# Weight slots 64 bytes off the 1024-byte grid of the activations, in a two-layer streaming-encoder kernel

## The chip, the cores and the metric

The kernel runs on one core of a Trainium2 chip. The time is device time in microseconds (us), the median of several executions. Before the change it is 1166.72 us, the median of 3 runs (1166.25 to 1168.82). The engines go by short names in the profile: PE is TensorE, PEld its weight loads, DVE VectorE, ACT ScalarE, POOL GpSimd, SP SyncE (whose queue issues most DMAs).

## The reference

A trunk of two layers over 512 positions of width 1024, everything in float32. Layer 0 mixes with a short gated convolution beside a sliding-window attention, layer 1 with a gated spatial unit beside a latent attention; each layer then has a SwiGLU feed-forward network (FFN) of hidden width 2816. Cut to its frame:

```python
for layer in range(DEPTH):                       # 2
    h = rmsnorm(x, mix_norm[layer])
    z = h @ (e_w_in if layer % 2 == 0 else o_w_in)[layer // 2]
    ...                                          # conv + window attention, or gating + latent attention
    y = jnp.concatenate([rmsnorm(ya, ...), rmsnorm(yb, ...)], axis=-1) @ w_out
    x = x + y
    h = rmsnorm(x, ffn_norm[layer])
    gate, up = jnp.split(h @ w_ffn_in[layer], 2, axis=-1)     # 1024 x 5632
    x = x + (jax.nn.silu(gate) * up) @ w_ffn_out[layer]       # 2816 x 1024
```

## The kernel before

Activations lie in SBUF with the feature on the partition and the 512 positions along the row, as tiles of 128 x 512 float32 (2048 bytes a row). Every large matrix product is made of three products of split numbers: a value is kept as `hi`, rounded to the type float32r, and `lo`, the rest, also float32r. `product` (lines 1505 to 1509) then adds hi x hi, hi x lo and lo x hi in the same PSUM bank. With the weights as the stationary operand (128 x 128) the moving one is a 128 x 512 tile of activations; in the loads `O_CV` and in the value half of `O_UKV` the roles are the other way round.

Weights come in 188 numbered loads of up to 1024 columns a row. For each, SyncE issues a DMA into one of two `raw` slots; ScalarE copies it, rounded, into one of four slots of `w_hi` (`hi`, line 651); VectorE subtracts and writes the same slot of `w_lo` (`lo`, line 1039); TensorE then uses it, in `load` (mostly 24 matmuls), and counts `load_used`, which frees the slot for load n + 4. ScalarE and VectorE each have their order of work written out by hand, with `through(p)` as the places at which splits are made. In the FFN (`ffn_in`, `ffn_out`) these are loops on every engine.

Other matmuls work in plain float32: `mean` (line 1538) sums squares over partitions with `ones` or a block matrix as the stationary operand, transposes (lines 1545, 1606, 1897, 1959) take the identity from the tile `small`, and the scores and values of the attentions are at lines 1596, 1618, 1882 and 1908.

Where tiles lie: `place[0]` begins at a multiple of 1024 bytes, and `sb` takes the next free place and rounds the size up to a multiple of 64. The order is xT, h_hi, h_lo, raw, w_hi, w_lo, then small, tables, gains, mix0_gain, gate_bias, sinks, eps_col, spare, mask_q, mask_k, tiny. Behind `tiny` the place is rounded up to a multiple of 1024 and row_scale, acc, sq, y0, rs follow; then, from R, the activations of the stages at offsets of whole kilobytes. The slots of `w_hi` and `w_lo` are 4096 bytes a row, so all of them begin at a multiple of 1024, and a stationary slice in them at a multiple of 512:

```python
base = (nc.sbuf_base + 1023) // 1024 * 1024
...
    place[0] += (n + 63) // 64 * 64
...
place[0] = (place[0] + 1023) // 1024 * 1024
row_scale = sb("row_scale", [P, S])
```

Of the kernel before, what the change touches and what calls it, by code (L numbers as in the profile page):

```python
# [106 lines left out]
def program(nc, x, mix_norm, ffn_norm, w_ffn_in, w_ffn_out, e_w_in, e_conv, e_q_gain, e_k_gain,  # L107
# [6 lines left out]
    place = [base]  # L114

    def at(name, shape, dt, offset):
        return nc.alloc_sbuf_tensor_at(name, shape, dt, offset=offset)

    def sb(name, shape, dt=F32, size=4):
        n = size  # L120
        for d in shape[1:]:
            n *= d
        t = at(name, shape, dt, place[0])
        place[0] += (n + 63) // 64 * 64
        return t
# [6 lines left out]
    out_tok = at("out_tok", [P, QT, D], F32, h_at)  # L132

    raw = sb("raw", [P, RAW_SLOTS, 1024])
    w_hi = sb("w_hi", [P, W_SLOTS, 1024], F32R)
    w_lo = sb("w_lo", [P, W_SLOTS, 1024], F32R)

# [1887 lines left out]
```

## Time and profile before

| | before |
|---|---|
| median of 3 runs | 1166.72 us (1166.25 to 1168.82) |
| profiled execution | 1169.08 us, span of the trace 1167.3 us |
| granted TensorE clock, mean | 0.993 |
| PE busy | 1135.6 us, 97% of the span |
| PEld busy | 904.8 us, 78% |
| DVE busy | 579.3 us, 50% |
| ACT busy | 440.7 us, 38% |
| POOL busy | 118.2 us, 10% |
| HBM read, written | 101.23 MB, 2.10 MB |

The profile is one execution. A matmul's record holds its way through the array too, so records overlap, and the busy time of PE says less than how far apart matmuls start. The ends of matmuls are modelled.

### The profile page before, as it was taken

What the parts mean: (1) busy time and instruction counts of PE and PEld (TensorE: products, weight loads), DVE (VectorE), ACT (ScalarE), POOL (GpSimd) and SP (SyncE); (2) the same over time, 40 slices, a digit from 0 to 9 for tenths busy, and PEclk for the clock granted to TensorE, in tenths of its full rate; (3) what the DMA queues carried; (4) which work ended last, traced back from release to release, by engine and by line L of the source; (5) the groups of instructions that cost most, each with busy time, mean ns of one, the idle gap of its engine ahead of it and who ended that gap; (6) DMA issues with size and microseconds to landing.
All of it is one profiled execution on the core that took longest, in us unless ns stands there. A gap on an engine that the chain in (4) does not pass through costs nothing.

```text
span 1167.3 us, 13729 instructions
## 1 busy us (share of the span) xinstructions
PE 1135.6 (97%) x5059; PEld 904.8 (78%) x5059; DVE 579.3 (50%) x796; ACT 440.7 (38%) x681; POOL 118.2 (10%) x154
## 2 busy tenths in 40 slices
PE   6999889999999999999999989999999999999998
PEld 5777678888888888888877745588888888888886
DVE  6578885533434433242665796565343343342321
ACT  5445444423323322131546666543332332331210
POOL 5010200001101000000204120000110110110000
PEclk9999999999999999999999998999999999999999
DMA  6522123233223232232323210023323323322230
GB/s 186 190 56 71 55 74 107 82 98 107 89 92 107 90 96 103 90 101 79 91 75 93 72 40 16 1 72 109 95 89 105 99 89 99 106 87 95 90 126 36
DMA packets 84983, 103.87 MB, mean 89 GB/s; under 512 B 10579, under 2 KB 61456, under 8 KB 84816
## 3 DMA queue, kind: packets, MB, share of 16 engines
q1 hardware_dynamic: 81792, 101.99, 28.0%
q10 hardware_dynamic: 2096, 1.05, 0.3%
q8 instruction: 25, 0.41, 0.2%
q0 software_dynamic: 1056, 0.30, 0.1%
q14 instruction: 14, 0.11, 0.0%
HBM read 101.23 MB, written 2.10 MB: 89 GB/s over the span
## 4 chain that ended last, share of the span: by engine, by line
PE 91%; DVE 6%; ACT 1%; DMA 1%; issue 1%; POOL 0%; ACTq 0%; DVEq 0%; POOLq 0%
PE ps L1507 27%; PE ps L1509 27%; PE ps L1508 27%; PE ps L1882 2%; PE ps L1538 2%; PE ps L1908 2%; DMA x_tok<-in_x 1%; PE ps L1897 1%; DVE e_sc L1188 1%; DVE e_pT L1196 1%; PE ps L1884 0%; DVE e_sc L1177 0%; DVE conv_y L1237 0%; DVE rs L1091 0%; PE ps L1959 0%
## 5 line engine op out<-in xcount | busy, mean ns | idle before, releaser
L1039 DVE TENSOR_TENSOR w_lo<-raw,w_hi 128x1024 fp32r<-128x1024 f32 (+2 forms) x194 | 227.9, 1180 | 445.2 <-ACT w_hi L651 442.1
L651 ACT ACTIVATE w_hi<-raw 128x1024 fp32r<-128x1024 f32 (+2 forms) x194 | 196.1, 1017 | 486.5 <-PE ps L1509 471.0
L1507 PE MATMUL ps<-h_hi,w_hi 128*128 128x512 f32 x928 | 368.2, 397 | 0.6 <-DVE conv_h L1208 0.6
L1509 PE MATMUL ps<-h_hi,w_lo 128*128 128x512 f32 x928 | 362.1, 390 | 0.0
L1508 PE MATMUL ps<-h_lo,w_hi 128*128 128x512 f32 x928 | 362.0, 390 | 0.0
L1507 PEld LDWEIGHTS ps<-h_hi,w_hi 128*128 128x128 f32 x928 | 174.9, 188 | 41.5 <-issue 4.6
L1508 PEld LDWEIGHTS ps<-h_lo,w_hi 128*128 128x128 f32 x928 | 174.9, 188 | 38.3 <-issue 2.6
L1509 PEld LDWEIGHTS ps<-h_hi,w_lo 128*128 128x128 f32 x928 | 174.6, 188 | 36.6
L1507 PE MATMUL ps<-act_hi,w_hi 128*128 (+1 forms) x352 | 137.1, 390 | 0.0
L1509 PE MATMUL ps<-act_hi,w_lo 128*128 (+1 forms) x352 | 137.1, 389 | 0.0
L1508 PE MATMUL ps<-act_lo,w_hi 128*128 (+1 forms) x352 | 137.0, 389 | 0.0
L544 POOL TENSOR_TENSOR ffn_t<-ffn_t,row_scale 128x512 f32<-128x512 f32 x40 | 50.9, 1293 | 555.6 <-ACT ffn_t L816 555.6
L1508 PEld LDWEIGHTS ps<-act_lo,w_hi 128*128 128x128 f32 x352 | 66.1, 188 | 13.8
L1507 PEld LDWEIGHTS ps<-act_hi,w_hi 128*128 128x128 f32 x352 | 66.1, 188 | 13.7
L1509 PEld LDWEIGHTS ps<-act_hi,w_lo 128*128 128x128 f32 x352 | 66.1, 188 | 13.6
L1291 DVE TENSOR_TENSOR ffn_t<-ps,ffn_t 128x512 f32<-128x512 f32 x44 | 30.4, 692 | 44.7 <-POOL ffn_t L544 40.7
L819 ACT ACTIVATE act_hi<-ffn_t 128x512 f32 (+1 forms) x44 | 27.9, 633 | 49.2 <-DVE ffn_t L1291 49.2
L816 ACT ACTIVATE ffn_t<-ffn_t 128x512 f32<-128x512 f32 x44 | 27.1, 632 | 39.0 <-DVE ffn_t L1287 39.0
L1294 DVE TENSOR_TENSOR act_lo<-ffn_t,act_hi 128x512 f32 (+1 forms) x44 | 30.2, 687 | 6.5 <-ACT act_hi L819 6.3
L1882 PE MATMUL ps<-o_k,o_q 128*128 128x512 f32 (+3 forms) x64 | 27.7, 517 | 4.6 <-ACT o_p L971 3.1
L1263 DVE TENSOR_TENSOR xT<-ps,xT 128x512 f32<-128x512 f32 x32 | 20.9, 684 | 19.4 <-PE ps L1509 19.4
L1287 DVE TENSOR_TENSOR ffn_t<-ps,row_scale 128x512 f32<-128x512 f32 x44 | 28.2, 682 | 0.0
(247 smaller groups left out, 1079.7 us busy)
## 6 DMA issues: line engine op xcount, KB each, us to landing
raw<-in_w_ffn_in SPq DMA_DIRECT2D x88, 512.0 KB, 3.5
raw<-in_w_ffn_out SPq DMA_DIRECT2D x44, 512.0 KB, 3.7
raw<-in_e_w_in SPq DMA_DIRECT2D x18, 512.0 KB, 3.6
raw<-in_o_w_in SPq DMA_DIRECT2D x8, 512.0 KB, 3.6
raw<-in_o_w_out SPq DMA_DIRECT2D x8, 512.0 KB, 3.6
raw<-in_e_w_out SPq DMA_DIRECT2D x8, 256.0 KB, 3.8
raw<-in_e_w_out SPq DMA_DIRECT2D x4, 512.0 KB, 3.9
out_dram<-out_tok SPq DMA_DIRECT2D x8, 256.0 KB, 3.6
```

The lines of the kernel that those rows point to most:

```text
L544: pool.tensor_tensor(ffn_t[:, t, :], ffn_t[:, t, :], row_scale[:, :], ALU.mult).then_inc(silu_scaled, 1)
L651: ins = act.activation(dst, src, ACT.Copy)
L816: act.activation(ffn_t[:, b, :], ffn_t[:, b, :], ACT.Silu).then_inc(silu_done, 1)
L819: act.activation(dst[:, t, :], ffn_t[:, (t0 + t) % 4, :], ACT.Copy).then_inc(hidden_hi, 1)
L1039: ins = TT(dst, src, high, ALU.subtract)
L1287: TT(ffn_t[:, (t0 + t) % 4, :], ps[:, b0 + t, :], row_scale[:, :], ALU.mult).then_inc(gate_scaled, 1)
L1291: TT(ffn_t[:, b, :], ps[:, b0 + 2 + t, :], ffn_t[:, b, :], ALU.mult).then_inc(hidden_ready, 1)
L1294: TT(dst_lo[:, t, :], ffn_t[:, (t0 + t) % 4, :], dst_hi[:, t, :].bitcast(F32), ALU.subtract).then_inc(hidden_lo, 1)
L1507: MM(dst, st_hi, mv_hi, start=start, stop=False)
L1508: MM(dst, st_hi, mv_lo, start=False, stop=False)
L1509: return MM(dst, st_lo, mv_hi, start=False, stop=stop)
L1882: MM(s_, o_q[:, h, i * P:(i + 1) * P], o_k[:, h, 0:P * (i + 1)], start=True, stop=False)
```

## The change

One line is added to the function that places the tiles: the place moves on by 64 bytes between `raw` and `w_hi`. `w_hi`, `w_lo` and the tiles that follow them up to `tiny` begin 64 bytes later; `row_scale` and all behind it stay, since the rounding ahead of it takes up the 64 bytes.

```diff
     raw = sb("raw", [P, RAW_SLOTS, 1024])
+    place[0] += 64
     w_hi = sb("w_hi", [P, W_SLOTS, 1024], F32R)
     w_lo = sb("w_lo", [P, W_SLOTS, 1024], F32R)
```

## Rows read from the trace of the kernel before

**Rows 1.** The page: busy times, then the chain by engine and by line.

```profile
PE 1135.6 (97%) x5059; PEld 904.8 (78%) x5059; DVE 579.3 (50%) x796; ACT 440.7 (38%) x681; POOL 118.2 (10%) x154
...
PE 91%; DVE 6%; ACT 1%; DMA 1%; issue 1%; POOL 0%; ACTq 0%; DVEq 0%; POOLq 0%
PE ps L1507 27%; PE ps L1509 27%; PE ps L1508 27%; PE ps L1882 2%; PE ps L1538 2%; PE ps L1908 2%; DMA x_tok<-in_x 1%; PE ps L1897 1%; DVE e_sc L1188 1%; DVE e_pT L1196 1%; PE ps L1884 0%; DVE e_sc L1177 0%; DVE conv_y L1237 0%; DVE rs L1091 0%; PE ps L1959 0%
```

**Rows 2.** One line's instructions, line 1509: launches, ns min/median/max, first and last start.

```profile
L1509 PE MATMUL ps<-h_hi,w_lo x928: 387/389/628, 16.2 to 1037.5; 128*128 128x512 f32 x186
...
L1509 PE MATMUL ps<-w_hi,h_lo x32: 388/390/398, 594.0 to 618.8; 128*128 128x512 f32 x32
...
L1509 PE MATMUL ps<-ckv_hi,w_lo x8: 387/389/396, 664.7 to 681.8; 128*128 128x512 f32 x8
```

**Rows 3.** Busy time by stage, PE alone: window, us, busy (count), clock, DMA.

```profile
250.00:520.00 270.00, 270.00 (x1193) 1.00 0.31 97
820.00:1080.00 260.00, 260.00 (x1149) 1.00 0.31 95
```

**Rows 4.** Instructions in order of time, steady FFN: start us, us, engine, line.

```profile
300.68 0.39 PE L1508 MATMUL ps<-h_lo,w_hi 128*128 128x512 f32 x1
300.68 0.19 PEld L1509 LDWEIGHTS ps<-h_hi,w_lo 128*128 128x128 f32 x1
```

**Rows 5.** Single matmuls by line (85.9, 1158.9, 669.6 us), and the weight load after 85.94.

```profile
L1508 PE MATMUL ps<-h_lo,w_hi 128*128 128x512 f32 x1 | 0.4, 390 | 0.0
L1509 PE MATMUL ps<-h_hi,w_lo 128*128 128x512 f32 x1 | 0.4, 388 | 0.0
...
L1508 PE MATMUL ps<-act_lo,w_hi 128*128 128x512 f32 x1 | 0.4, 389 | 0.0
L1509 PE MATMUL ps<-act_hi,w_lo 128*128 128x512 f32 x1 | 0.4, 389 | 0.0
...
L1508 PE MATMUL ps<-w_lo,ckv_hi 128*128 128x256 f32 x1 | 0.3, 283 | 0.0
L1509 PE MATMUL ps<-w_hi,ckv_lo 128*128 128x256 f32 x1 | 0.3, 279 | 0.0
...
88.71 0.50 PEld L1606 LDWEIGHTS ps<-small,e_sc 128*128 128x128 f32 x3 [2.80 <-issue]
```

**Rows 6.** Plain float32: lines 1538 and 1897 by tile, two means in order of time.

```profile
L1538 PE MATMUL ps<-acc,small x20: 589/591/668, 32.5 to 808.7; 128*128 128x512 f32 x20
L1897 PE MATMUL ps<-small,o_p x80: 272/273/332, 692.4 to 749.5; 128*128 128x128 f32 x80
...
209.11 1.02 PE L1538 MATMUL ps<-acc,small 128*128 128x512 f32 x2
```

**Rows 7.** After a plain matmul at 209.56: two of eight matmuls in order, one by line.

```profile
210.20 0.40 PE L1508 MATMUL ps<-h_lo,w_hi 128*128 128x512 f32 x1
...
211.82 0.39 PE L1509 MATMUL ps<-h_hi,w_lo 128*128 128x512 f32 x1
...
L1509 PE MATMUL ps<-h_hi,w_lo 128*128 128x512 f32 x1 | 0.4, 397 | 0.0
```

**Rows 8.** VectorE and ScalarE by line: launches, ns min/median/max, first and last start.

```profile
L1230 DVE SCALAR_TENSOR_TENSOR conv_y<-conv_h,gains,conv_y x4: 742/743/746, 123.0 to 125.0; 128x511 f32<-128x511 f32 x4
L1102 DVE SCALAR_TENSOR_TENSOR yb<-yb,gains,rs x4: 743/748/752, 147.8 to 153.5; 128x512 f32<-128x512 f32 x4
L1039 DVE TENSOR_TENSOR w_lo<-raw,w_hi x194: 685/1226/1842, 12.6 to 1138.7; 128x1024 fp32r<-128x1024 f32 x170, 128x512 fp32r<-128x512 f32 x12, 128x768 fp32r<-128x768 f32 x12
L651 ACT ACTIVATE w_hi<-raw x194: 611/1061/1070, 11.5 to 1137.6; 128x1024 fp32r<-128x1024 f32 x170, 128x512 fp32r<-128x512 f32 x12, 128x768 fp32r<-128x768 f32 x12
```

**Rows 9.** The start in order of time, and the DMA issues by line (KB, us to landing).

```profile
0.76 0.40 SPq L373 DMA_DIRECT2D small<-const_small  x1
7.03 3.46 PE L1545 MATMUL ps<-small,x_tok 128*128 128x128 f32 x16 [7.03 <-DMA x_tok<-in_x]
...
small<-const_small SPq DMA_DIRECT2D x1, 128.0 KB, 3.4
```

## The prediction

> **What bounds the kernel now.** I read the chain that ended last first: TensorE is 91% of it, and the three matmul lines of `product` carry 27% each, VectorE only 6% [rows 1]. So what the change can be worth is decided by one number, how far apart two of those matmuls start. The view of line 1509 counts them: its ten groups, from 928 launches down to 8, add up to 1488; lines 1507 and 1508 are issued beside it each time, so 4464 launches in all, nearly all with 512 columns [rows 2]. Next, the busy time by stage: 270 us of the first FFN hold 1193 matmuls and 260 us of the second 1149, each count including two that begin before the window, at full clock with no idle [rows 3]. That is 270 / 1191 = 226.7 ns and 260 / 1147 = 226.7 ns from start to start. 512 columns at 2.4 GHz are 213.3 ns, so 13.3 ns of each interval are not columns: 4464 x 13.3 = 59 us of the kernel. Whether these 13.3 ns have to do with where the operands lie is the whole question.
>
> In this stretch the load of the next stationary tile begins together with a matmul's stream: the load at 300.68 with the matmul at 300.68, and so on, 0.19 us long [rows 4]. Both then read SBUF. The stationary tile is a slice of a weight slot, the moving one a tile of the activations. Before, slots and activations all begin at multiples of 1024 bytes and slices step by 512 bytes, so the two reads begin 0 or 512 bytes apart modulo 1024; after, 64 or 576.
>
> **The change, part by part.** No instruction, wait or transfer is added, removed or put in another order. What moves by 64 bytes is w_hi, w_lo and all that `sb` places behind them down to `tiny`: the constants with identity and ones, tables, gains, the bias and sink tiles, the masks. The tail behind `w_lo` has 576 bytes modulo 1024, with the 64 it has 640, and the rounding ahead of `row_scale` takes up both: from `row_scale` on every address is the same.
>
> The weight load against the stream. The test is a matmul beside which no weight load runs. At 85.94 us a 512-column one ends its weight slot's work, and the next weight load comes at 88.71 us: it lasts 388 ns, the one before it, with a weight load beside it, 390. At 1158.93 us, again with nothing behind it, it is 389 after 389. With 256 columns, the last of its stage lasts 279 ns, the one before it 283 [rows 5]. A collision of the two reads is thus worth 0 to 2 ns in a 512-column stream and some 4 ns in a 256-column one, not 13. Where do the 13 come from? They belong to this kind of matmul, and an address of the stationary tile has nothing to do with them. The rest, 2 to 3 ns, is about what lies between two plain fp32 matmuls: two of them take 1.02 us together, the second begins 1.02 - 0.59 = 0.43 us after the first, for 0.427 us of columns [rows 6].
>
> So the gain is bounded by 1.5 ns (389.5 against 388) on 4464 matmuls, 6.7 us, if 64 bytes end all collision; by 4 ns, 18 us, if the 256-column case is the true size of it. The trace also has the other side. After a pause or a plain matmul the intervals are longer for a while: from 210.20 us to 211.82 us seven of them take 1.62 us, 231.4 ns each, and one of these matmuls lasts 397 ns; then the 226.7 ns return [rows 7]. The addresses in those eight are the same as in the steady stretch, so what differs is how the two streams stand to each other in time. If the shift kept them in that state, each interval would cost 4.8 ns more: 4464 x 4.8 = 21 us. I take nothing for either: zero is nearest to the long stretches, in which tiles 0 and 512 bytes apart follow each other and two engines write in between, and 1191 intervals in a row have one length.
>
> Here the Trainium skill can be weighed. SBUF — State Buffer, section "Who interferes with whom", gives TensorE two independent read ports and says that it never waits for anyone; by it the sum is zero. The 283 against 279 ns do not agree to the last nanosecond, by which the page's zero and the 18 us above differ; no row tells whether those 4 ns hang on the address.
>
> The engines that write the slots. In the FFN a load is 24 matmuls or 5.4 us of TensorE, and its split is one ScalarE copy of 1.06 us and one VectorE subtraction of 1.23 us [rows 8]: even if both took twice as long, TensorE would hide them. In the first 200 us and around the attention VectorE stands in the chain with 6%. There an operand that begins 4 bytes off costs nothing: 743 ns for 511 elements at line 1230, against 748 ns for 512 aligned ones at line 1102 [rows 8]. Zero, and if each subtraction for the 26 loads ahead of the first FFN lost 10 ns, 0.3 us.
>
> The constants as moving or stationary operands: transposes read the identity, the means the ones, at 64 instead of 0 or 512. The largest group, 80 transposes at line 1897, would move by 0.4 us at 5 ns each [rows 6]; the others are smaller.
>
> The transfers into shifted tiles: the first, 128 KB of `small`, is issued at 0.76 us and lands 3.4 us later, at 4.2; TensorE starts at 7.03 us when x arrives [rows 9]. 2.8 us of cover; without it, a start that is late by a few tenths. The tables are used 600 us later. Nothing.
>
> Sum: 0 us, against the profiled execution's 1169.1 us (span 1167.3 and 1.8 around it), which is 2.4 us over the median of the three runs; on the median, 1166.7 us.
>
> **The rivals.** First: the shift does end collisions, a little. For it: 279 against 283 ns. Against it: 388 against 389 and 390, and that 0 and 512 bytes make no difference now. 4.5 to 18 us less, 1149 to 1162 us.
>
> Second: the 13.3 ns are a conflict of two reads that begin alike, after all, and the lone matmul only looks as long since the ends of matmuls are modelled. Then an interval would fall to the overhead of a plain matmul, 3 ns over its columns: 10 ns x 4464 = 45 us, 1122 us. Against it: with weights as the moving operand the median is 390 ns, with weights as the stationary one 389 [rows 2], whichever of the two reads is the one from the slot. The Trainium skill, TensorE: Matmul & The Clock Gate, section "Back-to-back issue gap", has 2.5 ns over the columns for a warm matmul, where this trace has 13.3; taken as a rule for this kind too it would put the gain at 10.8 ns x 4464 = 48 us.
>
> Third, the slower side: place, the intervals inside every load; mechanism, a stationary tile that begins 64 bytes further meets the faster stream a little later, and the even pace of 226.7 ns gives way to that after a restart. Price 4.8 ns x 4464 = 21 us, 1188 us, or 1 to 1.5 ns and 1171 to 1173 us when only the collisions double. It decides from the point at which an interval in the FFN is longer than 227.2 ns (2.3 us over the kernel). Against it: the record of a weight load is 0.19 us long in 0.227 us, so it isn't what an interval waits for [rows 4].
>
> That the change does nothing it says is no rival: the addresses do move.
>
> **How the numbers follow.** No difference 0.64, with its own range of 1164.4 to 1169.1 us. First rival 0.14 (0.09 of it above 1160 us), second 0.05, third 0.17 (0.08 of it up to 1174 us). A measurement of this kernel can tell about 0.2% (2.3 us) from no change: faster 0.19, same 0.64, slower 0.17. The range from 1160 to 1174 us holds 0.64 + 0.09 + 0.08 = 0.81.
>
> **What would show it.** In the profile after, 270 us of the first FFN should hold 1193 matmuls again; 1198 or more would mean that collisions cost and are gone, 1188 or fewer the third rival. The 512-column records should keep their median of 389 ns, the weight loads 188, and the lone one 388. Two intervals that alternate between even and odd slices (0 and 512 bytes) would show an effect of the address even where their sum stays. The prediction is wrong at its root if the lone record and the interval shrink together: then the 11 ns were not this matmul's own.

## The result

The changed kernel takes 1193.91 us (median of 4 runs, 1193.43 to 1194.37) against 1167.77 us for the kernel before in the same comparison (4 runs): a ratio of 1.0224, 95% interval 1.0212 to 1.0236. It is slower by 26 us, outside the range of the prediction. Place and sign are those of its third rival: every interval inside the loads is longer.

The profiled execution after took 1193.57 us with a span of 1191.8 us, 24.5 us over the span before. (The profiled execution before was 1.3 us over its own median, so this difference is smaller than the 26 us between the medians.) The page after, engines and chain (all line numbers are one higher than before), to be held against [rows 1]:

```profile
PE 1161.2 (97%) x5059; PEld 904.7 (76%) x5059; DVE 579.4 (49%) x796; ACT 440.8 (37%) x681; POOL 118.6 (10%) x154
...
PE 90%; DVE 6%; ACT 2%; DMA 1%; issue 1%; POOL 0%; ACTq 0%; DVEq 0%; POOLq 0%
```

The instruction counts are the same, DVE, ACT and PEld are as busy as before to within 0.1 us, and PE alone has 25.6 us more. Nobody waits for anything new. The busy time by stage, PE alone, the windows of [rows 3]:

```profile
250.00:520.00 270.00, 270.00 (x1158) 1.00 0.30 93
820.00:1080.00 260.00, 260.00 (x1115) 1.00 0.30 94
```

There were 1193 and 1149 matmuls in these windows. One of the 1158 began before its window: 270 / 1157 = 233.4 ns from start to start, and 233.3 from the single starts, against 226.7. Of the 1115 two did: 260 / 1113 = 233.6 ns, a little more because this window now holds the two plain matmuls of a mean, at 822.64 us, and the restart behind them. The single matmuls in order of time, start and length in us, in the steady first FFN:

```profile
299.76 0.40 PE L1508 MATMUL ps<-h_hi,w_hi 128*128 128x512 f32 x1
300.00 0.39 PE L1509 MATMUL ps<-h_lo,w_hi 128*128 128x512 f32 x1
300.23 0.40 PE L1510 MATMUL ps<-h_hi,w_lo 128*128 128x512 f32 x1
300.47 0.39 PE L1508 MATMUL ps<-h_hi,w_hi 128*128 128x512 f32 x1
...
302.10 0.40 PE L1509 MATMUL ps<-h_lo,w_hi 128*128 128x512 f32 x1
```

Records of 0.40 and 0.39 us take turns: in nanoseconds 398 and 393, with intervals of 236 and 231, over and over, 233.3 ns in the mean. From 300.00 to 302.10 us there are nine intervals. (At the end of the second FFN every record is 394 and every interval 233 or 234, the same mean by another pattern.) Before, the records were 389 or 390 and every interval 226 to 228.

Where the 24.5 us lie, from the first matmuls of the loads that bound each stage, in order of time in both traces:

| stage | before, us | after, us | more |
|---|---|---|---|
| up to the end of the first output projection | 198.2 | 200.2 | 2.0 |
| first FFN, 1584 matmuls | 359.9 | 370.5 | 10.5 |
| odd layer's input projections | 106.0 | 107.8 | 1.7 |
| attention, second part | 85.3 | 84.1 | -1.2 |
| second output projection | 47.9 | 48.9 | 1.0 |
| second FFN, 1584 matmuls | 361.5 | 372.0 | 10.5 |

1584 x 6.67 ns are 10.6 us: each FFN is explained to 0.1 us by the interval alone. All 4464 at that price would be 29.8 us; outside the FFNs less is lost, and the traces show several reasons, whose shares were not separated. Part of the loss disappears in waits. Before, the restarts after pauses had longer intervals than 226.7 ns already. And in the four loads in which the weights are the moving operand the interval is not 233 ns but, once settled, 228.9, here eight intervals in 1.83 us:

```profile
608.94 0.39 PE L1508 MATMUL ps<-w_hi,h_hi 128*128 128x512 f32 x1
...
610.77 0.39 PE L1510 MATMUL ps<-w_hi,h_lo 128*128 128x512 f32 x1
```

There the stationary slice lies 64 bytes below the moving tile, which is 192 modulo 256; the experiments below find the same 228.9 ns at 192 bytes.

The -1.2 us of the attention can't be put down to the addresses. In both executions TensorE's clock fell to its lower level, 1.2 GHz, in this stage. Ahead of the fall TensorE had been waiting part of the time (before it was busy for 3.8 of 6.0 us, after for 12.2 of 16.8). Two windows around the low clock, before and then after; the third figure from the end is the granted clock, which makes some 10 us at the lower level before and 7 us after:

```profile
696.00:707.00 11.00, 10.11 (x20) 0.53 0.15 48
...
712.80:719.70 6.90, 6.90 (x15) 0.51 0.20 76
```

### The profile page after: what moved, and what is told of

Its sections match the earlier page's. It is cut to its first block, busy times and chain, and to the rows that moved or that the text cites. A ratio compares the mean times of both kernels' runs of the same rounds, so it can differ in the third digit from the quotient of the medians.

```text
span 1191.8 us, 13729 instructions
## 1 busy us (share of the span) xinstructions
PE 1161.2 (97%) x5059; PEld 904.7 (76%) x5059; DVE 579.4 (49%) x796; ACT 440.8 (37%) x681; POOL 118.6 (10%) x154
## 4 chain that ended last, share of the span: by engine, by line
PE 90%; DVE 6%; ACT 2%; DMA 1%; issue 1%; POOL 0%; ACTq 0%; DVEq 0%; POOLq 0%
PE ps L1508 27%; PE ps L1510 27%; PE ps L1509 27%; PE ps L1883 2%; PE ps L1539 2%; PE ps L1909 1%; DMA x_tok<-in_x 1%; DVE e_sc L1189 1%; PE ps L1898 1%; ACT e_sc L740 1%; DVE e_sc L1178 1%; DVE tiny L1170 1%; PE ps L1885 0%; DVE e_pT L1197 0%; DVE conv_y L1238 0%
## 5 line engine op out<-in xcount | busy, mean ns | idle before, releaser
L1508 PE MATMUL ps<-h_hi,w_hi 128*128 128x512 f32 x928 | 373.1, 402 | 0.6 <-DVE conv_h L1209 0.6
L1510 PE MATMUL ps<-h_hi,w_lo 128*128 128x512 f32 x928 | 367.2, 396 | 0.0
L1509 PE MATMUL ps<-h_lo,w_hi 128*128 128x512 f32 x928 | 367.2, 396 | 0.0
L1508 PEld LDWEIGHTS ps<-h_hi,w_hi 128*128 128x128 f32 x928 | 174.7, 188 | 47.2 <-issue 4.6
```

The source lines that it names most:

```text
L1508: MM(dst, st_hi, mv_hi, start=start, stop=False)
L1509: MM(dst, st_hi, mv_lo, start=False, stop=False)
L1510: return MM(dst, st_lo, mv_hi, start=False, stop=stop)
```

## The experiments

Three theories were open. **A**: the distance between the stationary slice and the moving tile decides. **B**: a weight slot off the 1024-byte grid is slow by itself. **C**: other engines or the shifted constants are the cause.

### Whole kernels: constants alone, everything alike

```diff
     w_lo = sb("w_lo", [P, W_SLOTS, 1024], F32R)
+    place[0] += 64
```

> The 64 bytes are put behind w_lo instead of ahead of w_hi: only the constants and small tiles move, the weight slots stay on the 1024-byte grid. If the weight slots are the cause (theories A and B), the time is that of before, 1166 to 1169 us, and the FFN interval 226.7 ns. If the shifted identity, ones, tables or gains were the cause, it is that of after, about 1194 us.

Measured: 1167.98 us, ratio 1.0005 (0.9994 to 1.0016); 1193 matmuls in the 270 us window. Moving identity, ones, tables and gains costs nothing that can be measured.

```diff
-    base = (nc.sbuf_base + 1023) // 1024 * 1024
+    base = (nc.sbuf_base + 1023) // 1024 * 1024 + 64
...
-    place[0] = (place[0] + 1023) // 1024 * 1024
+    place[0] = (place[0] + 959) // 1024 * 1024 + 64
```

> Everything is shifted by 64 bytes, weight slots and activations alike, so that the distance between them is 0 or 512 modulo 1024 as before, and both begin at 64. Theory A (the distance decides): 1166 to 1169 us, interval 226.7 ns. Theory B (slots off the grid are slow by themselves): about 1194 us, interval 233.3 ns.

Measured: 1169.08 us, ratio 1.0012 (1.0000 to 1.0024), the window again:

```profile
250.00:520.00 270.00, 270.00 (x1193) 1.00 0.32 97
```

The slots are off the grid as in the changed kernel, and the time is that of before. B has fallen, and so has any theory about where ScalarE and VectorE write the slots: what decides is the distance between slots and activations.

### Whole kernels: other distances

The same one-line edit as the change, with another number of bytes.

> Slots 192 bytes off the grid: 228.9 ns in TensorE alone. Theory A, the full kernel has the same interval: 4464 x 2.2 = 10 us more, 1175 to 1179 us. If the grid of 1024 bytes decided (theory B): as after, 1194 us.

> Slots 256 bytes off the grid. Theory A with a period of 256 bytes, as TensorE alone showed it: the time of before, 1166 to 1169 us. With a period of 1024 bytes: between the two.

> Slots 128 bytes off the grid. TensorE alone has 232.4 ns there for one offset, 233.3 with slices 512 bytes apart in one of two runs of the stretch. If the interval alone sets the time (theory A): 1187 to 1194 us, FFN interval 232.4 to 233.3 ns. Theory B (only 64 is bad): 1167 us.

```diff
     w_hi = sb("w_hi", [P, W_SLOTS, 1024], F32R)
+    place[0] += 64
     w_lo = sb("w_lo", [P, W_SLOTS, 1024], F32R)
```

> Only the slots of w_lo are 64 bytes off, those of w_hi stay on the grid. In TensorE alone with the lo slices 64 bytes apart from the hi ones the mean interval was 231.1 ns. Theory A (each matmul pays by the distance of the slice that is loaded beside it, with what the one before left over): 231.1 ns, 4464 x 4.4 = 20 us more at most, 1182 to 1187 us. If each launch paid by its own slice alone, one in three would be at 233.3: 228.9 ns and 1175 to 1177 us.

The windows of 250 to 520 us with the slots at 192, 256 and 128 bytes and with w_lo alone at 64, in this order:

```profile
250.00:520.00 270.00, 270.00 (x1181) 1.00 0.30 95
...
250.00:520.00 270.00, 270.00 (x1192) 1.00 0.31 97
...
250.00:520.00 270.00, 270.00 (x1164) 1.00 0.30 92
...
250.00:520.00 270.00, 270.00 (x1170) 1.00 0.30 94
```

| slots at, bytes | FFN interval from the single starts, ns | time, us | ratio (95% interval) |
|---|---|---|---|
| 64 (the change) | 233.3 | 1193.91 | 1.0224 (1.0212 to 1.0236) |
| 128 | 232.4 | 1191.46 | 1.0205 (1.0176 to 1.0235) |
| 192 | 228.9 | 1174.79 | 1.0066 (1.0049 to 1.0083) |
| 256 | 226.7 | 1167.03 | 0.9999 (0.9987 to 1.0011) |
| w_lo alone at 64 | 231.1 | 1185.37 | 1.0153 (1.0124 to 1.0183) |

Three of the four times came where expected; with 192 bytes the interval did, and the time is 7.8 us over its comparison instead of 10, just under the stated band; as with the change, less is lost outside the FFNs. What counts is the distance modulo 256 bytes, not 1024. With w_lo alone, a third of the stationary slices is shifted and the kernel pays 18 us of the 26: the launches don't pay each for itself.

### TensorE alone: the distance

A kernel in which TensorE alone multiplies split tiles of x, 72 matmuls for each distance, after one plain fp32 matmul. The rest of the computation is left out. Its core (one such line for each stretch):

```diff
+        for o, st, mv, f, l in plan(64, 0, 1024, 512): ins = MM(o, st, mv, start=f, stop=l)
```

> This kernel leaves the whole computation out: TensorE alone multiplies split tiles of x, in 33 stretches of 72 matmuls in the order of product(), with a plain fp32 matmul between stretches; only the byte offsets of the stationary slices (s) and of the moving tile (m) differ. First 16 stretches: all slices at one offset, s = 0, 64, ... 960 modulo 1024, m = 0. Then 12 with slices stepping by 512 bytes as in the kernel, s = 0, 16, 32, 48, 64, 96, 128, 192, 256, 320, 384, 448. Then (s, m) = (64, 64), (0, 64), (0, 960), and two stretches of 256 columns with s = 0 and 64. Theory A, the distance between the stationary slice and the moving tile decides: s = 64, step 512 gives 233.3 ns from start to start (records of 393 to 398 ns), s = 0 gives 226.7 (389), (64, 64) gives 226.7 again, and (0, 960), which has the same distance as (64, 0), gives 233.3. Theory B, a stationary slice off the 1024-byte grid is slow by itself: (64, 64) gives 233.3 like (64, 0), and (0, 64), (0, 960) give 226.7. Theory C, the pace comes from other engines' traffic in the kernel and not from TensorE's own reads: all stretches have one interval.

One line's instructions for some stretches: launches, ns min/median/max, first and last start in us. In order: slices at 0, 64, 128, 192 and 256 bytes, then slice and tile both at 64, then 256 columns with slices at 0 and at 64:

```profile
L165 PE MATMUL ps<-split_a,split_w x72: 387/389/793, 40.1 to 56.6; 128*128 128x512 f32 x72
L167 PE MATMUL ps<-split_a,split_w x72: 393/398/798, 57.3 to 74.3; 128*128 128x512 f32 x72
L169 PE MATMUL ps<-split_a,split_w x72: 388/393/798, 74.9 to 91.9; 128*128 128x512 f32 x72
L171 PE MATMUL ps<-split_a,split_w x72: 388/392/798, 92.5 to 109.2; 128*128 128x512 f32 x72
L173 PE MATMUL ps<-split_a,split_w x72: 387/389/799, 109.9 to 126.4; 128*128 128x512 f32 x72
...
L221 PE MATMUL ps<-split_a,split_w x72: 387/389/801, 529.3 to 545.9; 128*128 128x512 f32 x72
...
L227 PE MATMUL ps<-split_a,split_w x72: 278/283/685, 581.6 to 590.5; 128*128 128x256 f32 x72
L229 PE MATMUL ps<-split_a,split_w x72: 276/276/682, 591.0 to 599.5; 128*128 128x256 f32 x72
```

The median record tells the distance: 389 at 0 and 256, 398 and 393 by turns at 64. The starts give the intervals: after the first interval, of 0.63 us, 70 intervals take 15.9 us at 0 and 16.3 us at 64. Taken from the single starts, once settled: 226.67 ns at 0, 233.33 at 64, 232.4 at 128, 228.9 at 192, and the same four numbers (within 0.1 ns) at 256 + these, 512 + these and 768 + these. In these sixteen stretches all slices lie at one offset. With slices that step by 512 bytes as in the kernel, 32 and 48 bytes gave 233.33 and 96 bytes 234.3, and a stretch at 128 bytes settled at 233.33 where the one at 384 had 232.4. Slice and tile both at 64 give 226.67; tile at 960 and slice at 0, which is 64 apart, 233.33; tile at 64 and slice at 0, which is 192 apart, 228.9. No other engine works during the stretches, so C has fallen too. With 256 columns the order is reversed: 120.0 ns at 0 and 113.3 ns at 64.

The lengths of the records add nothing to this. Here and in the whole kernels a split matmul's record is the interval to the next start plus some 162 ns: 389 with 226.7, 398 with 236, 393 with 231, 283 with 120.0, 276 with 113.3.

### TensorE alone: what is under the 226.7 ns

> The computation is left out again, TensorE alone, 28 stretches of 72 matmuls. Now finer offsets of the stationary slices (8, 16, 24, 32, 208, 224, 240, 248 bytes), the lo slices 16, 64 or 128 bytes apart from the hi ones, and slices that take every second or fourth column, so that a weight load walks through SBUF at another speed than before. Theory A1 (the stream and the weight load walk through the same 256 bytes at two speeds and collide each time the faster passes the slower): an ordinary slice never gets below 226.7 ns, wherever it begins, since it is always passed; a slice of every second column, which walks as fast as the stream, keeps its distance and is either always or never in the way: at some offset the interval falls to about 216 ns, at others it is above 226.7. Theory A2 (what is over the columns belongs to this kind of matmul, and only 64, 128 and 192 bytes add to it): slices of every second column have 226.7 ns at best, as ordinary ones.

One line's instructions for three stretches: slices at 16 bytes behind a stretch at 8, at 16 bytes behind a stretch at 0, and slices of every second column that begin at 0:

```profile
L172 PE MATMUL ps<-split_a,split_w x72: 387/395/796, 74.2 to 91.1; 128*128 128x512 f32 x72
...
L222 PE MATMUL ps<-split_a,split_w x72: 389/389/792, 514.2 to 530.7; 128*128 128x512 f32 x72
...
L196 PE MATMUL ps<-split_a,split_w x72: 392/394/799, 284.6 to 301.5; 128*128 128x512 f32 x72
```

The fall that A1 expected didn't come: slices of every second column have 230.0 to 233.3 ns at all eight offsets, of every fourth 235.0 to 240.0. None is below 226.67. It isn't a clean test, though, for in these stretches the four slices begin 4 bytes apart instead of 512, so none holds a single distance, and 8 bytes alone cost ordinary slices 4 ns: they have 230.6 ns there. At 240 bytes ordinary slices have 226.67. At 16 bytes they have 226.67 in one stretch of this kernel and 233.33 in another, with nothing different but what ran before. Over all kernels of this kind, the three stretches at 16 bytes that came behind one at 0 settled at 226.67, the three that came behind one at 8 or 64 bytes at 233.33, each time with a plain fp32 matmul in between. (A whole kernel with its slots at 16 bytes, expected at 1165.5 to 1168 us if the distance decides, gave no result, so which pace it would take isn't known.)

> The computation is left out, TensorE alone. Stationary slices of 96, 64 and 32 columns (a shorter weight load) at 0 and 64 bytes; moving tiles of 384, 256 and 128 columns; bf16 at 0, 64, 128, 192 bytes; plain fp32 at 0 and 64; a stretch at 16 bytes after four different ones; then trains of 1, 2, 3, 4, 8 and 9 split matmuls of which the last runs with no weight load beside it, at 0, 64 and 192 bytes. Theory A1 (all that is over 213.3 ns is the collision of the stream with the next weight load): shorter weight loads bring the interval down at both offsets, towards 216 ns with 32 columns; a lone matmul (train of 1) has the same record at every offset. Theory A2 (11 to 13 ns belong to the kind of matmul, the load beside it only adds at a bad distance): with 32 columns 64 bytes give 226.7 ns as well, and 0 bytes stay at 226.7. Both: the last of a long train lasts longer at 64 bytes (397 ns in the changed kernel) than at 0 (388), though no load runs beside it; if that is carried over from the loads before it, trains of 1 don't differ by offset and longer ones do. Plain fp32 takes two cycles a column and doesn't change with the offset.

One line's instructions: slices of 32 columns at 64 bytes; bf16 at 0 and 64 bytes; plain fp32 at 0 and 64; then the last matmul, with no weight load beside it, of trains of 2, 3 and 8 at 0 bytes, and of 8 at 64 bytes:

```profile
L189 PE MATMUL ps<-split_a,split_w x72: 391/396/791, 135.3 to 152.2; 128*32 128x512 f32 x72
...
L203 PE MATMUL ps<-half_a,half_w x70: 379/379/379, 216.6 to 231.7; 128*128 128x512 bf16 x70
L205 PE MATMUL ps<-half_a,half_w x71: 379/379/379, 232.8 to 248.1; 128*128 128x512 bf16 x71
L211 PE MATMUL ps<-x_tok x144: 592/592/592, 282.0 to 343.3; 128*128 128x512 f32 x144
L213 PE MATMUL ps<-x_tok x144: 592/592/593, 344.6 to 406.0; 128*128 128x512 f32 x144
...
L233 PE MATMUL ps<-split_a,split_w x6: 388/397/397, 516.5 to 520.4; 128*128 128x512 f32 x6
L237 PE MATMUL ps<-split_a,split_w x6: 397/397/397, 522.3 to 527.5; 128*128 128x512 f32 x6
...
L245 PE MATMUL ps<-split_a,split_w x6: 388/388/388, 538.9 to 549.7; 128*128 128x512 f32 x6
...
L269 PE MATMUL ps<-split_a,split_w x6: 390/390/390, 593.3 to 604.3; 128*128 128x512 f32 x6
```

Three things follow. First, shorter weight loads don't help: 96, 64 and 32 stationary columns at 0 bytes give 230.0, 230.0 and 231.7 ns, at 64 bytes 228.3, 232.6 and 231.7. So neither theory was right as written: a collision in proportion to the length of the load doesn't fit, but 0 bytes didn't stay at 226.7 either. Second, bf16 at 0, 64, 128 and 192 bytes and plain fp32 at 0 and 64 have one record each (215.8 and 429.2 ns from start to start): of the three kinds only the float32r matmul shows the effect. It depends on the moving columns as well: with 384 of them 0 and 64 bytes give 173.3 and 174.7 ns, with 256 again 120.0 and 113.3, with 128 both give 111.7. Third, the last matmul of a train, with no load beside it, lasts anything from 388 to 397 ns at 0 bytes, by the length of the train and in part among trains of one length, and at 64 bytes 390 ns behind seven others and 397 behind eight. (Trains of one begin after a pause and last 495 ns or more at each distance.) Its length goes with what the train left behind, not with whether a load runs beside it.

> The computation is left out, TensorE alone, 28 stretches. The moving lo tile 16 to 240 bytes further than the hi one; the lo slices 32 to 240 bytes further than the hi ones; the order of the three products changed (hh lh hl, hl hh lh, hh alone) at slices 0 and 64; slices all at 32, 96, 160, 224; one slice over and over; both lo parts moved alike. Theory A (a launch pays by the distance, modulo 256 bytes, between its moving tile and the slice that is loaded beside it): in order hh hl lh the hi tile streams beside a hi load and a hi load again, the lo tile beside a lo load; so both lo parts moved alike by 64, 128 or 192 keep every distance and give 226.7 ns, while either alone gives 228 to 233; the order alone changes nothing at 0. Theory D (226.7 ns is no floor but one of several paces that a row of matmuls can settle in, and the distance only chooses between them): some setting here is below 226.7 ns.

Here h and l name the hi and lo parts, the stationary one first; the kernel's own order is hh hl lh. One line's instructions: order hh lh hl at 0 bytes, then both lo parts moved alike by 64 and by 192 bytes:

```profile
L194 PE MATMUL ps<-split_a,split_w x72: 387/389/799, 266.8 to 283.4; 128*128 128x512 f32 x72
...
L218 PE MATMUL ps<-split_a,split_w x72: 391/394/798, 477.0 to 493.8; 128*128 128x512 f32 x72
...
L222 PE MATMUL ps<-split_a,split_w x72: 388/395/796, 512.0 to 529.0; 128*128 128x512 f32 x72
```

Theory A in the form "a launch pays by the distance to the slice that is loaded beside it" has fallen: both lo parts moved alike give 231.1 (64 bytes), 231.1 (128) and 233.3 ns (192), though each pair keeps its distance. D expected a pace below 226.67 ns in some setting and has found none in the 28 stretches. What stands is coarser. With 128 stationary columns, all operands at one offset modulo 256 bytes give 226.67 ns, whatever the order of the three products (227 after 227, also with one slice over and over), and nearly everything else tried with slices of adjacent columns, but for offsets of 16 and 240 bytes, gives 228 to 235. The layout of the kernel before is at the best pace that any experiment found, so no faster version came out of them.

## Why the prediction was wrong

**The bound.** Right: TensorE's interval is the whole story, and reading it from the counts per window was enough to see the loss in the profile after.

**What moves and what doesn't.** Right for the constants, the first transfer and the engines that write the slots, each costed at zero: with the constants alone shifted the ratio is 1.0005.

**The step that failed** is the test with the lone matmul. It took 388 ns without a weight load against 390 with one [rows 5] as the worth of a collision, 0 to 2 ns, and from that concluded that "an address of the stationary tile has nothing to do with them". The comparison holds one distance fixed, 0 or 512 bytes, which are one and the same modulo 256; it can't tell what another distance does. The runs show 6.7 ns in each interval at 64 bytes in place of this step's zero. And the record doesn't measure what it was taken to measure. The lone one after, at 1183.41 us with no weight load behind it:

```profile
L1510 PE MATMUL ps<-act_hi,w_lo 128*128 128x512 f32 x1 | 0.4, 397 | 0.0
L1509 PE MATMUL ps<-act_lo,w_hi 128*128 128x512 f32 x1 | 0.4, 394 | 0.0
```

It is 397 ns long with nothing beside it, and trains at 0 bytes end with 388 as well as 397. A lone record depends on the row of matmuls before it. If the 162 ns between record and interval hold for it as well, which no next start can confirm, the lone one after took 235 ns with nothing beside it, more than the 233 ns of the two before it, which had a load beside them. The difference between a record with a load beside it and one without is then not what the load costs.

**That tiles 0 and 512 bytes apart make no difference now** was true, and was read as insensitivity to distance. It only shows that the period divides 512. Two samples that the layout itself ties to one another are one sample.

**The third rival** had place and sign, and of the mechanism what can be seen: the even pace gives way to intervals like those that the trace of before shows after a pause [rows 7]. That the shift keeps the row in the very state of a restart isn't shown; the intervals of a restart run from 224 to 236 ns, the settled ones are 231 and 236 by turns. Its price, 4.8 ns from that stretch, was too low: the interval settled 6.7 ns up, and 1188 us became 1193.9. Of the intervals after a pause, 231.4 ns were the mean over seven unequal ones; the longest there, 236 ns, is one of the two that now take turns. Its chance of 0.17 was too low for the same reason as above. The point from which it decides (227.2 ns) and its mark in the profile (1188 matmuls or fewer in 270 us; there are 1158) came out on the right side. The mark of even and odd slices taking turns says less than the prediction made of it: the turns of 231 and 236 ns come with all slices at one offset too, so they belong to the row and not to the slices.

**The 13.3 ns.** That most of it belongs to this kind of matmul stands so far: with 512 moving columns no distance, order, stride or shorter load brought it down. That it is this matmul's own and untouched by addresses was half wrong: the floor wasn't touched, but there is a second part above it that is.

**The second rival** (226.7 falls to some 216 ns) found no support: in over ninety stretches of split matmuls with 512 columns none settled below 226.67 ns. With 256 columns 64 bytes do gain, 120.0 to 113.3 ns, but the kernel has 48 of those, and in them the weights move, so that the distance is 192: they went from 120 to 118 ns. The Trainium skill's zero (SBUF — State Buffer, "Who interferes with whom": TensorE has two independent read ports and never waits for anyone) can't be taken to mean that the place of one operand is free: here 64 bytes cost 26 us. Whether one read waits for the other no run shows. The Trainium skill's 2.5 ns over the columns for a warm matmul (TensorE: Matmul & The Clock Gate, "Back-to-back issue gap") agree with 215.8 ns for bf16, and with 429.2 for plain fp32 if that takes two cycles a column; they don't agree with float32r.

**What stays open.** Why the distance chooses the pace. The runs show that TensorE alone is enough; that, when all slices have one offset and all moving tiles another, the distance counts and counts modulo 256 bytes; that the distance of each pair doesn't explain the pace when hi and lo parts lie at different offsets; that something carries over from what ran before (16 bytes settled at 226.67 in three stretches and at 233.33 in three others); and that the pace doesn't follow the weight load's length. Which part of the chip keeps that state no run here shows.

## What to carry to other kernels

For float32r matmuls with 512 moving columns, put stationary and moving tiles at the same offset modulo 256 bytes, the lo parts as well: in the whole kernels and in TensorE alone that gave the best pace found. Aligning costs at most some padding, and a small tile in front of a weight buffer can cost 2% by itself. When a TensorE-bound kernel changes its time and no instruction did, count the matmuls in a fixed window before looking at anything else. And to argue that an address doesn't matter, look at which distances the trace holds: multiples of 512 bytes alone say nothing of 64.

## What the runs showed of the hardware that was not expected

- A row of float32r matmuls with 512 moving columns settles in a pace that repeats: 226.67 ns from start to start at distance 0, 233.33 at 64, 232.4 at 128, 228.9 at 192 bytes, period 256 bytes (128 also settled at 233.33 once); bf16 has 215.8 and plain fp32 429.2 at 0 and at 64.
- With 256 columns it is the other way round: 120.0 ns at 0, 113.3 at 64.
- At 16 bytes there are two settled paces, 226.67 and 233.33 ns, and what ran before decides between them.
- Rows with stationary slices of every second or fourth column, 4 bytes apart, take 230 to 240 ns; slices of 32 columns, at 231.7 ns, are no faster than those of 128.
- The record of the last matmul in a train varies from 388 to 397 ns at 0 bytes with no weight load beside it. Other records of split matmuls are some 162 ns over the interval to the next start.
